# Attention of a second block: bias tables added on VectorE with the row maximum, two units of scores in PSUM, output product unit by unit, weights scaled on Pool

## What is computed

```python
def hybrid_layer(h, ...):
    z = rms_norm_2(h, norm_g) @ w_in                # q, k, v, gate for 8 forgetting and 8 dilated heads of 64
    oa = forgetting_attention(qa, ka, va, log_f)    # s = q k^T/8 + c_i - c_j, causal; softmax; @ v
    ob = dilated_attention(qb, kb, vb)              # three dilated windows, merged by their log-sum-exps
    h = h + concat([oa * silu(ga), ob * silu(gb)]) @ w_out
    return h + (p_i @ w_ple) * sigmoid(rms_norm_2(h, ple_norm_g) @ w_ple_gate)
```

## Time and profile before

| | us |
|---|---|
| median of 3 runs | 3405.22 (3402.64 to 3407.63) |
| profiled execution, its own time | 3405.67 |
| its span in the profile | 3404.0 |

### The profile page before, as it was taken

The page is one execution under the profiler, slowest core; times in us unless marked ns, Lnnn a source line. Parts: engine busy times, 40 slices in busy tenths (PEclk is TensorE's granted clock), DMA queues, the critical chain, the costliest instruction groups (busy, mean ns, idle before and its releaser), DMA issues.

```text
span 3404.0 us, 38903 instructions
## 1 busy us (share of the span) xinstructions
PE 3301.3 (97%) x16560; PEld 2713.6 (80%) x16560; DVE 1675.1 (49%) x2150; ACT 1351.9 (40%) x1775; POOL 62.5 (2%) x112
## 2 busy tenths in 40 slices
PE   8999999899999999999999899999999999999999
PEld 7888887888688888888887888688888875888767
DVE  5443358644544434443348654444434456544564
ACT  5222248333432223222237523332224447444563
POOL 0000001100000000000001100000000000000000
PEclk9999999999999999999999999999999999999999
DMA  4222211022122222222221013122222220222102
GB/s 168 90 89 101 94 73 50 26 75 101 54 93 99 88 98 102 96 95 94 96 75 62 26 50 112 50 99 99 92 94 95 85 85 1 80 88 86 62 20 87
DMA packets 46892, 275.01 MB, mean 81 GB/s; under 512 B 5248, under 2 KB 8576, under 8 KB 21504
## 3 DMA queue, kind: packets, MB, share of 16 engines
q1 hardware_dynamic: 46720, 272.53, 22.6%
HBM read 270.41 MB, written 2.10 MB: 80 GB/s over the span
## 4 chain that ended last, share of the span: by engine, by line
PE 88%; DVE 5%; ACT 5%; issue 2%; DMA 0%; DVEq 0%; SPq 0%; ACTq 0%
PE banks L295 74%; PE banks L1383 2%; PE banks L1538 1%; PE banks L1552 1%; PE banks L1550 1%; ACT slab_hi L277 1%; PE banks L2367 1%; PE banks L2159 1%; ACT weights L2401 1%; PE banks L1002 1%; DVE sb_softplus L1770 1%; DVE slab_lo L284 1%; PE banks L1419 1%; PE banks L2358 1%; DVE weights_turned L2459 1%
## 5 line engine op out<-in xcount | busy, mean ns | idle before, releaser
L295 PE MATMUL banks<-x_hi,slab_hi 128*128 128x512 f32 x2688 | 1059.7, 394 | 12.1 <-DVE x_lo L376 12.1
L295 PE MATMUL banks<-x_hi,slab_lo 128*128 128x512 f32 x2688 | 1046.9, 389 | 0.0
L295 PE MATMUL banks<-x_lo,slab_hi 128*128 128x512 f32 x2688 | 1046.5, 389 | 0.0
L277 ACT ACTIVATE slab_hi<-slab_raw 128x2048 fp32r<-128x2048 f32 (+2 forms) x276 | 483.8, 1753 | 1074.1 <-PE banks L295 1064.9
L284 DVE TENSOR_TENSOR slab_lo<-slab_raw,slab_hi 128x2048 fp32r<-128x2048 f32 (+2 forms) x276 | 577.1, 2091 | 421.0 <-ACT slab_hi L277 421.0
L295 PEld LDWEIGHTS banks<-x_hi,slab_hi 128*128 128x128 f32 x2688 | 505.1, 188 | 123.4 <-issue 19.5
L295 PEld LDWEIGHTS banks<-x_lo,slab_hi 128*128 128x128 f32 x2688 | 505.2, 188 | 109.1 <-issue 5.7
L295 PEld LDWEIGHTS banks<-x_hi,slab_lo 128*128 128x128 f32 x2688 | 504.9, 188 | 105.5
L295 PE MATMUL banks<-hidden_hi,slab_hi 128*128 128x512 f32 x704 | 273.9, 389 | 0.0
L295 PE MATMUL banks<-hidden_lo,slab_hi 128*128 128x512 f32 x704 | 273.9, 389 | 0.0
L295 PE MATMUL banks<-hidden_hi,slab_lo 128*128 128x512 f32 x704 | 273.9, 389 | 0.0
(11 more groups left out here) (366 smaller groups left out, 4121.8 us busy)
## 6 DMA issues: line engine op xcount, KB each, us to landing
slab_raw<-slabs SPq DMA_DIRECT2D x196, 1024.0 KB, 4.8
slab_raw<-slabs SPq DMA_DIRECT2D x64, 704.0 KB, 4.0
slab_raw<-slabs SPq DMA_DIRECT2D x16, 640.0 KB, 3.8
h<-xT SPq DMA_DIRECT2D x8, 256.0 KB, 6.0
memory<-memT SPq DMA_DIRECT2D x2, 1024.0 KB, 5.5
out<-h SPq DMA_DIRECT2D x8, 256.0 KB, 4.3
constants<-con SPq DMA_DIRECT2D x1, 1412.5 KB, 10.5
memory_in<-memT SPq DMA_DIRECT2D x1, 1024.0 KB, 14.9
```

The lines of the kernel that those rows point to most:

```text
L277: self.nc.scalar.activation(self.wh[:, g % self.HIGHS, 0:w], self.raw[:, g % self.RAWS, 0:w], ACT.Copy).then_inc(self.hi_ready, 1)
L295: mm = self.nc.tensor.matmul(out, left[a], right[c], start=start and n == 0, stop=stop and n == 2)
```

## The change

`AttendPairs` is rewritten in these points. (1) The causal mask and the dilated table are no longer products: VectorE's `top` adds the table out of SBUF to the scores in PSUM, negates, writes the result to the SBUF weights and keeps the minimum, in one instruction per block and head; only the key sums stay a product. It waits until the weights' former unit is turned. (2) ScalarE's `exp` reads SBUF, with scale -1. (3) Scores have two bank pairs (banks 0 to 3), turned weights three banks (4 to 6), kept copies are plain and two units deep. (4) `keep` copies head 0 on VectorE and head 1 on ScalarE. (5) `out` runs per unit, one unit behind, in products of 128 columns. (6) The scaling is on Pool. (7) The first unit's scores wait for two banks less. (8) `BiasTables` makes a wide causal table and the picker alone.

```diff
     def bank(self, u, c):
-        n = u % self.UNITS
-        return self.k.ps[:, 2 * n + c, 0:self.WIDTH[n]]
+        return self.k.ps[:, 2 * (u % 2) + c, 0:self.WIDTH[u % self.UNITS]]
+
+    def turned(self, u, c):
+        return self.k.ps[:, 4 + (2 * u + c) % 3, 0:self.WIDTH[u % self.UNITS]]
+
+    def kept(self, u, c):
+        return self.pt[:, 2 * (u % 2) + c, 0:self.WIDTH[u % self.UNITS]]
...
         def score(u):
-            if u >= self.UNITS:
-                pe.wait_ge(*self.exp_done.at(2 * (u - 2)))
+            if u >= 2:
+                pe.wait_ge(*self.neg_ready.at(2 * (u - 1)))
...
-            pe.wait_ge(*self.p_ready.at(2 * u + 1 + c))
-            if u >= 1:
-                pe.wait_ge(*(self.pt_a, self.pt_b)[c].at(u))
-            if c and u % self.UNITS == 0 and u >= 1:
-                pe.wait_ge(*self.y_ready.at(u // self.UNITS))
+            pe.wait_ge(*self.p_ready.at(2 * u + c + 1))
+            if c and u >= 1:
+                pe.wait_ge(*self.pt_a.at(u))
+            elif u >= 2:
+                pe.wait_ge(*self.pt_b.at(u - 1))
...
-            for b in range(TB):
-                for c in range(2):
-                    col = c * self.HEAD + b * self.STEP
-                    mm = nc.tensor.matmul(ps[64 * c:64 * c + 64, self.OUT, b * P:S], self.value(p, c, b),
-                                          self.pt[:, col + b * P:col + S],
+        def out(u):
+            p, n = divmod(u, self.UNITS)
+            pe.wait_ge(*self.pt_a.at(u + 1))
+            pe.wait_ge(*self.pt_b.at(u + 1))
+            if n == 0 and p >= 1:
+                pe.wait_ge(*self.y_ready.at(p))
+            for tb, at in self.blocks(u):
+                for b in range(tb + 1):
+                    for c in range(2):
+                        mm = nc.tensor.matmul(k.ps[64 * c:64 * c + 64, self.OUT, tb * P:(tb + 1) * P],
+                                              self.value(p, c, b), self.kept(u, c)[:, at][:, b * P:(b + 1) * P],
+                                              start=tb == 0, stop=b == tb, skip_group_check=True)
...
+        pe.wait_ge(k.bank_free, self.banks_ready - 2)
+        score(0)
         pe.wait_ge(k.bank_free, self.banks_ready)
+        score(1)
+        score(2)
         for u in range(units):
             turn(u, 0)
             if u + 3 < units:
                 score(u + 3)
             turn(u, 1)
+            if u >= 1:
+                out(u - 1)
+        out(units - 1)
+
+    def gpsimd(self, pool):
+        for u in range(HEADS2 * self.UNITS):
+            pool.wait_ge(*self.inv_ready.at(u + 1))
+            for c in range(2):
+                for tb, at in self.blocks(u):
+                    w = self.weights(u, c)[:, at]
+                    ins = self.k.nc.gpsimd.tensor_scalar(w, w, self.col(self.ri, tb, c), None, ALU.mult)
+                ins.then_inc(self.p_ready.sem, 1)
...
         def exp(u):
-            act.wait_ge(*self.neg_ready.at(u + 1))
             for c in range(2):
+                act.wait_ge(*self.neg_ready.at(2 * u + c + 1))
                 for tb, at in self.blocks(u):
+                    w = self.weights(u, c)[:, at]
+                    ins = nc.scalar.activation(w, w, ACT.Exp, scale=-1.0, bias=self.col(self.nm, tb, c),
+                                               accum_out=self.col(self.sm, tb, c))
...
+        def keep(u):
+            act.wait_ge(*self.turn_done.at(2 * u + 2))
+            if u >= 2:
+                act.wait_ge(*self.part_ready.at(u - 1))
+            nc.scalar.activation(self.kept(u, 1), self.turned(u, 1), ACT.Copy).then_inc(self.pt_b.sem, 1)
...
-        scale(0)
         for u in range(units):
-            if u + 1 < units:
-                scale(u + 1)
             if u + 2 < units:
                 exp(u + 2)
+            keep(u)
...
         def top(u):
             dve.wait_ge(*self.z_ready.at(u + 1))
             if u >= 3:
+                dve.wait_ge(*self.turn_done.at(2 * (u - 2)))
                 dve.wait_ge(*self.exp_done.at(2 * (u - 2)))
-                ins = nc.vector.tensor_reduce(self.nm[:, 2 * tb:2 * tb + 2], ps[:, n:n + 2, at], AX.X, ALU.max,
-                                              negate=True)
+            for c in range(2):
+                for tb, at in self.blocks(u):
+                    ins = nc.vector.tensor_tensor_reduce(self.weights(u, c)[:, at], self.bank(u, c)[:, at],
+                                                         self.table(u // self.UNITS)[:, S - (tb + 1) * P:S],
+                                                         -1.0, 3e38, ALU.add, ALU.min,
+                                                         accum_out=self.col(self.nm, tb, c))
+                ins.then_inc(self.neg_ready.sem, 1)
...
+        def keep(u):
+            dve.wait_ge(*self.turn_done.at(2 * u + 1))
+            if u >= 2:
+                dve.wait_ge(*self.part_ready.at(u - 1))
+            nc.vector.tensor_copy(self.kept(u, 0), self.turned(u, 0)).then_inc(self.pt_a.sem, 1)
...
         for u in range(units):
             p, n = divmod(u, self.UNITS)
+            keep(u)
+            if u + 3 < units:
+                top(u + 3)
+            if u + 2 < units:
+                invert(u + 2)
             if n == 0 and p >= 1:
                 take(p - 1)
...
         def bias(out, p, n, c):
             if p < H // 2:
-                at, rest = (0, P, P)[n], (0, P, 2 * P)[n]
+                at, wide = (0, P, P)[n], (384, 384, 512)[n]
                 pick = tables.pick[:, 2 * p + c:2 * p + c + 1]
-                add(out, pick.broadcast_to([P, P]), self.key_sum[:, at:at + wide])
-                return add(out[:, rest:wide], tables.ident[:], tables.causal[:, 0 if n == 0 else P:3 * P])
-            at = (3 * P, P, 0)[n]
-            add(out, tables.ident[:], tables.dil_hi[:, at:at + wide])
-            return add(out, tables.ident[:], tables.dil_lo[:, at:at + wide])
+                return add(out, pick.broadcast_to([P, P]), self.key_sum[:, at:at + wide])
+            return None
+
+        def table(p):
+            return tables.causal[:] if p < H // 2 else tables.dilated
```

More of the change, by code:

```diff
@@ L2294, in __init__ @@
         self.z_ready = Signal(k, "attend_z", 24)
[L2295 removed]
+        self.neg_ready = Signal(k, "attend_neg", 48)
         self.exp_done = Signal(k, "attend_exp", 48)
@@ L2372, in tensor @@
+        pe.wait_ge(k.bank_free, self.banks_ready - 2)
+        score(0)
         pe.wait_ge(k.bank_free, self.banks_ready)
-        for u in range(3):
-            score(u)
-            add_bias(u)
+        score(1)
+        score(2)
         for u in range(units):
-            first = u % self.UNITS == 0 and u >= 1
-            if first:
-                out(u // self.UNITS - 1)
             turn(u, 0)
```

104 lines of the change are left out of this document (26 added, 78 removed).

## The result

The changed kernel takes 3378.18 us (median of four runs, 3377.08 to 3379.34) beside 3404.36 us for the kernel before (four runs); the ratio is 0.992, with a 95% interval from 0.9904 to 0.9936. The forecast was 3377 us, 3362 to 3398. It had started from the profiled execution of the kernel before, 3405.67 us; between the medians the saving is 26.2 us, between the two profiled executions 27.7, where 29 was forecast. The changed kernel's profiled execution took 3377.94 us, its span is 3375.9, 28.1 less than before.

The account below looks back on a forecast made before the run. TensorE was taken as the bound, with a small leak of waits. Shorter periods (13.6 us) and head (0.9) save 14.5 us a stage, 29 for two: 3405.7 - 29 = 3377 us, range 3362 to 3398.

Parts of the forecast that it names:

- Bias: TensorE's bias products in the attention stages: dropping them saves 2.4 us net a dilated pair, 0.75 a forgetting pair.
- The dilated period as a whole: Time of a dilated head pair in the attention stages, set by TensorE: from 11.05 to 8.6 us.
- Output by unit: TensorE's output products in 128-column pieces, three starts a pair: +0.35 us for starts, +0.2 for switches among transposes.
- rival C: Weight loads show in TensorE's output products, 0.20 us a step: no gain, 3406 us; chance 0.07.
- Rival B: VectorE becomes the bound, its fused add-and-minimum taking two cycles per element: period about 10.3 us, 3391 us; chance 0.12.
- Pool: the step that failed: Pool takes over the scaling, eight instructions a pair: 4.5 us taken, bounds 3.5 to 6.4, under the 8.6 us period.
- The loop: Transposes, maximum, reciprocal and Pool's scaling in turn: 4.5 to 5.0 us per two dilated units against TensorE's 5.7; fits.
- Head: Start of an attention stage: first transposes at about 2809.5 where they were at 2810.37, so -0.9 us.
- Tail: Last three units of an attention stage, transposes and output steps without scores: 7.1 us.
- Clock: TensorE's lower clock level after the idle head stays in both attention stages, some 1.7 us lost in the first.
- Rival D: Pool and VectorE shut each other out in the attention stages: period some 12 us, 3418 us; chance 0.08.
- Rival E: TensorE's lower clock level strikes outside the head, in half of the 14 full periods: 46 us, 3423 us; chance 0.03.

Follow-up runs that it names:

- the extra dose: Changed kernel with six more 32-column Pool instructions a pair, one ahead of each half's scaling: 3398.99 us, ratio 0.9985.
- the doses on VectorE: Changed kernel with one more VectorE sum of 384 columns a unit: one operand in PSUM, 3384.59 us; both in SBUF, 3390.92 us.

## Why the prediction was right

The sum came out within about 1 us of the median, and most terms did, but one resource was priced far off without harm to the periods, and misses of a few us cancelled. Per stage, head and tail took some 2.9 us more than forecast and the periods some 0.9 less; the second stage gave back about 1.6 by its clock, 1.1 us came from outside the stages, and the forecast had started from an execution 1.3 us above the median that the result is compared with. That the total came out so close is luck; that TensorE's shorter work sets the periods is not.

- **Bias.** Net -2.4 a dilated pair, from streamed columns and switches. Put back, it costs 2.47. Right. Read start to start, the three pieces with their switches took 2.86 us in a dilated pair of the kernel before (0.82, 0.86 and 1.18); part of what went with them came back in the transposes, below.
- **The dilated period as a whole.** TensorE's 10.40 us without the wait became 8.48, so -1.92 where the forecast had -1.85. By pieces it is -2.86 for the bias, +0.58 for the transposes and +0.35 for the output.
- **Output by unit.** Three starts for one, +0.35: 2.65 against 2.33 us. Steps at 0.11, not 0.20: rival C fell. The transposes took a little more than the 0.2 and 0.3 of switches put on them: 3.07 us a pair where they took 2.49 in the kernel before (by the same reading, start to start), +0.58. Dilated period 8.48 against the forecast's 8.6, forgetting 9.77 against 9.9 (its terms add up to 9.95).
- **VectorE.** Forecast 7.1 us a pair, 6.6 busy. The fused instruction lasts 688 ns at 512 columns, against about 0.7; the reads, put at 0.7 us a pair, add nothing, since the next instruction starts with them. Rival B needed two cycles per element and fell: from 290 ns at 128 columns to 688 at 512 it is 1.04 ns a column, as in the copies. The rule of the Trainium skill that I weighed (Vector Engine (DVE) Microarchitecture Reference, § Points that are easy to get wrong) speaks of two SBUF sources. These rows, with one source in PSUM, don't contradict it and don't test it.
- **ScalarE.** Forecast 6.5, busy 6.67. Right as busy time. With the scaling back on it, ScalarE is full at 9.73 us, 3.6 of them scaling, so start to start its own work takes 6.1.
- **Pool: the step that failed.** The bounds were 3.5 to 6.4 us a pair and I took 4.5; it is 8.49 start to start, outside both. The lower bound came from a memset and from selects, the upper from a two-operand product, whose 1272 ns for 512 columns I divided by its columns. Two things were wrong. I held one operand to be cheaper than two, but the scaling of 512 columns takes 1560 ns, 23% more than that product. And a whole time divided by its columns hides the part that each instruction costs whatever its width: from 128 to 512 columns the scalings start 0.58 to 1.54 us apart, which is 2.5 ns a column and 0.26 us beside them. For the eight of a pair that makes 2560 x 2.5 ns = 6.4 us and 8 x 0.26 = 2.1. That the first figure is the old upper bound is chance. The periods stood because TensorE's own 8.48 was just as long. That is luck: had Pool been slower, or VectorE's low part fallen elsewhere, it would have been the bound, as the extra dose shows one for one, and the shifted low part at 0.33 us a pair.
- **The loop.** It fitted, but with less to spare than the 0.7 to 1.2 us that I counted, Pool's half being 1.2 to 1.6 us and not 0.6 to 1.1. No run closed it by the link that the forecast named, the maximum waiting for transposes. With the output once a pair the rest of it, maximum, reciprocal, Pool, was held up by a copy that waited for its buffer.
- **Head.** Forecast -0.9; from the last product of line 295 to the first transposes it is 9.05 us in both stages where it was 9.27 (2801.10 to 2810.37): -0.2. That the first transposes come at 2809.42, as forecast (2809.5), is chance: the stage began 0.73 us earlier, and from profile to profile its start moves by more than that (2798.54 to 2803.06 in the runs up to the doses on VectorE). Pool's first half is 1.5 us where I took 0.6 to 1.1.
- **Tail.** Forecast 7.1 us for the last three units; it is 9.3 (2873.72 to 2883.06). The difference is the four waits for Pool, 2.28 us. The same error in Pool's price, at the two places where TensorE has nothing else to do.
- **Clock.** I kept the loss of the slow head in both stages. It fell away in the second (mean 1.00), which gave back part of what Pool took: the first stage saved 12.0 us, the second 15.0, where 14.5 each were forecast. That is chance, not insight: only 2 of 22 unfilled heads are without it, and in another profile of this kernel both stages have it.
- **Rival D** had 0.08 and a period of some 12 us. The mechanism is there (the low part and a scaling that starts within it), but the price is 0.2 to 0.4 us a meeting, and only instructions with both operands in SBUF had it. The Trainium skill, SBUF — State Buffer, § Who interferes with whom, separates the two cases by the number of SBUF inputs; the two VectorE doses agree with it: 0.83 us a pair between them.
- **Rival E** didn't come in the steady periods (clock 1.00 in all of them). With the output once a pair it did come into them: the granted clock is 0.50 from 2863.20 to 2866.40, after a wait of 1.76 us, though not after the wait of 1.77 in the period before.

## What to carry to other kernels

When an edit moves work to an engine that has been idle, price it by its slope and by a fixed part per instruction, and ask what happens if it is twice the estimate; if the answer is "it ties with the bound", the estimate needs a row of its own. An engine full in a steady period costs nothing there, but its latency shows at head and tail, where the bound has nothing to fill in; splitting the moved work over two engines with time to spare took back most of it here. And where a copy waits for a product, count what is queued behind the copy: with buffers for three units, cutting the product into units cost 0.3 us of starts and saved waits of 1.8 us a pair.

## What the runs showed of the hardware that I had not expected

- Pool's multiplication of fp32 in place by a value per partition: 1560, 1240, 921 and 600 ns at 512, 384, 256 and 128 columns (286 ns at 32 columns by a constant, 0.39 us by a value per partition). That is 2.5 ns a column and some 0.3 us beside them, and at 512 columns it is slower than the two-operand product, 1272 ns.
- ScalarE does the same work in 0.61, 0.51, 0.40 and 0.29 us start to start (3.6 us for two of each), its durations being 0.1 longer.
- A Pool instruction that starts while VectorE works on two SBUF operands is held up by 0.2 to 0.4 us. One under way, or one beside a VectorE instruction with an operand in PSUM, is not; but a VectorE instruction with two SBUF operands that starts 0.10 to 0.15 us behind a Pool instruction is itself longer by 0.2 to 0.3 us.
- TensorE's lower clock level came after the idle span of 2.7 to 3.2 us at the head of a stage in 20 of 22 heads, and in none of six whose idle spans were filled with transposes. The same kernel shows both (mean 0.96 and 1.00 over its two stages).
